# Weight splits in two halves of 1024 columns with a signal each, in a four-block transformer kernel on one core

## The reference, cut to what matters

```python
def hierarchical_moe(h, w_group, b_group, w_expert, b_expert, w_gate, w_up, w_down):
    ...
        gate = jnp.einsum('td,edf->tef', xb, w_gate)
        up = jnp.einsum('td,edf->tef', xb, w_up)
        act = jax.nn.silu(gate) * up * cb[..., None].astype(xb.dtype)
        return jnp.einsum('tef,efd->td', act, w_down)
```

## Time and profile before

| | |
|---|---|
| median of 3 runs | 1689.23 us (1687.36 to 1690.05) |
| the profiled execution's own time | 1690.0 us |
| its span, first to last instruction | 1688.0 us |
| TensorE busy | 1531.2 us, 91% |
| VectorE busy | 1295.4 us, 77% |
| ScalarE busy | 995.6 us, 59% |
| mean granted clock of TensorE | 0.959 of full speed |
| read from HBM | 400.37 MB, 238 GB/s over the span |

### The profile page before, as it was taken

How to read it: one execution, slowest core, us unless ns; L and a number is a source line. 1 busy time by engine, 2 the same in 40 slices (tenths; PEclk the granted TensorE clock), 3 DMA queues, 4 the chain that set the end, 5 groups by cost and what they waited for, 6 DMA issues and landing times.

```text
span 1688.0 us, 20547 instructions
## 1 busy us (share of the span) xinstructions
PE 1531.2 (91%) x7230; PEld 1257.6 (75%) x7230; DVE 1295.4 (77%) x1578; ACT 995.6 (59%) x1126; POOL 95.7 (6%) x187
## 2 busy tenths in 40 slices
PE   5997999979898899979969999999798969999998
PEld 4776877858776678768857888788686758888786
DVE  6756899776657898874667899888675578988877
ACT  3543577644534666646345777767385437777665
POOL 4002000030022000000020000000000100000000
PEclk9998999979998999989988999999799979999999
DMA  9433599865434799844445999999542228999985
GB/s 315 141 106 115 184 335 339 287 219 179 139 118 150 261 328 346 285 159 141 150 153 181 368 352 360 357 317 349 170 144 75 87 92 291 358 362 358 360 301 211
DMA packets 282868, 402.77 MB, mean 239 GB/s; under 512 B 16026, under 2 KB 220538, under 8 KB 282512
## 3 DMA queue, kind: packets, MB, share of 16 engines
q1 hardware_dynamic: 273632, 381.99, 66.9%
q0 software_dynamic: 9136, 19.48, 3.7%
HBM read 400.37 MB, written 1.05 MB: 238 GB/s over the span
## 4 chain that ended last, share of the span: by engine, by line
PE 69%; DVE 15%; ACT 6%; DMA 4%; issue 4%; SPq 0%; DVEq 0%; ACTq 0%
PE bank L623 19%; PE bank L625 18%; PE bank L624 18%; DVE w_lo_at L1920 5%; ACT w_hi_at L1384 3%; PE bank L640 2%; DMA raw_at<-in_moe_w_up_dram 2%; PE bank L755 1%; DMA raw_at<-in_moe_w_down_dram 1%; PE bank L780 1%; PE bank L911 1%; DMA raw_at<-in_w_in_dram 1%; PE bank L665 1%; DVE t_lo_at L1927 1%; PE bank L667 1%
## 5 line engine op out<-in xcount | busy, mean ns | idle before, releaser
L1920 DVE TENSOR_TENSOR w_lo_at<-raw_at,w_hi_at 128x2048 fp32r<-128x2048 f32 (+1 forms) x365 | 828.3, 2274 | 156.3 <-ACT w_hi_at L1384 147.5
L1384 ACT ACTIVATE w_hi_at<-raw_at 128x2048 fp32r<-128x2048 f32 (+1 forms) x365 | 693.4, 1901 | 176.3 <-PE bank L625 123.1
L623 PE MATMUL bank<-w_hi_at,xs_hi_at 128*128 128x512 f32 x800 | 327.4, 409 | 25.7 <-DVE w_lo_at L1920 12.5
L625 PE MATMUL bank<-w_hi_at,xs_lo_at 128*128 128x512 f32 x800 | 318.1, 398 | 0.0
L624 PE MATMUL bank<-w_lo_at,xs_hi_at 128*128 128x512 f32 x800 | 316.1, 395 | 0.0
L623 PE MATMUL bank<-w_hi_at,t_hi_at 128*128 128x512 f32 (+3 forms) x528 | 210.1, 398 | 12.2 <-DVE t_lo_at L1927 5.2
L624 PE MATMUL bank<-w_lo_at,t_hi_at 128*128 128x512 f32 (+3 forms) x528 | 203.8, 386 | 0.0
L625 PE MATMUL bank<-w_hi_at,t_lo_at 128*128 128x512 f32 (+3 forms) x528 | 203.7, 386 | 0.0
L623 PEld LDWEIGHTS bank<-w_hi_at,xs_hi_at 128*128 128x128 f32 x800 | 152.9, 191 | 59.1 <-DVE w_lo_at L1920 17.2
L625 PEld LDWEIGHTS bank<-w_hi_at,xs_lo_at 128*128 128x128 f32 x800 | 152.6, 191 | 34.9
L624 PEld LDWEIGHTS bank<-w_lo_at,xs_hi_at 128*128 128x128 f32 x800 | 153.4, 192 | 30.7
(11 more groups left out here) (500 smaller groups left out, 1726.6 us busy)
## 6 DMA issues: line engine op xcount, KB each, us to landing
raw_at<-in_moe_w_dram SPq DMA_DIRECT2D x192, 512.0 KB, 5.3
raw_at<-in_moe_w_gate_dram SPq DMA_DIRECT2D x128, 512.0 KB, 5.1
raw_at<-in_moe_w_up_dram SPq DMA_DIRECT2D x128, 512.0 KB, 6.5
raw_at<-in_moe_w_down_dram SPq DMA_DIRECT2D x128, 512.0 KB, 5.3
raw_at<-in_w_in_dram SPq DMA_DIRECT2D x40, 512.0 KB, 6.0
raw_at<-in_a_w_in_dram SPq DMA_DIRECT2D x20, 512.0 KB, 4.7
raw_at<-in_w_out_dram SPq DMA_DIRECT2D x16, 512.0 KB, 4.2
raw_at<-in_ple_wg_dram SPq DMA_DIRECT2D x16, 512.0 KB, 4.8
```

Of the source, the lines that this page charges most:

```text
L623: pe.matmul(out, ah, bh, start=start, stop=False, skip_group_check=loose)
L625: return pe.matmul(out, al, bh, start=False, stop=stop, skip_group_check=loose)
L1384: act.activation(WH[:, s.part(), 0:width], RAW[:, s.slot(), 0:width], ACT.Copy).then_inc(hi_done, 1)
L1920: dve.tensor_tensor(WL[:, s.part(), 0:width], RAW[:, s.slot(), 0:width], WH[:, s.part(), 0:width].bitcast(F32), ALU.subtract).then_inc(spl ...
```

## The change

Each split is made in two operations of half the unit's columns, on ScalarE and on VectorE. `hi_done` and `split_done` become two signals each, one for either half. TensorE waits for the first half's signal where it waited for the unit, and for the second half's ahead of the unit's third chunk. SyncE waits for the second half's signal. The other users of units (`unit_by_channel`, `down`, `down_by_half`, the mixing of heads, the projection of `p`, `unit_kv`) are changed in the same way.

```diff
-        hi_done = sem("hi_done")
-        split_done = sem("split_done")
+        hi_half = [sem(f"hi_half{i}") for i in range(2)]
+        split_half = [sem(f"split_half{i}") for i in range(2)]
...
                 if not s.early(1 - RING):
-                    sp.wait_ge(split_done, s.count(1 - RING))
+                    sp.wait_ge(split_half[1], s.count(1 - RING))
...
             def unit_by_token(banks, chunk, first, last, w=512, mid=None, src=(TH, TL)):
                 hi, lo = src
-                pe.wait_ge(split_done, s.count(1))
+                pe.wait_ge(split_half[0], s.count(1))
                 for c in range(4):
                     if c == 2 and mid is not None:
                         mid()
+                    if c == 2:
+                        pe.wait_ge(split_half[1], s.count(1))
...
                 def up(e, half, x, cols=slice(0, P)):
-                    pe.wait_ge(split_done, s.count(1))
+                    pe.wait_ge(split_half[0], s.count(1))
                     for k in range(4):
+                        if k == 2:
+                            pe.wait_ge(split_half[1], s.count(1))
...
                 def down(p, e):
                     pe.wait_ge(*m.al.at(p, e))
-                    pe.wait_ge(split_done, s.count(1))
+                    pe.wait_ge(split_half[0], s.count(1))
                     for f in range(2):
+                        if f == 1:
+                            pe.wait_ge(split_half[1], s.count(1))
...
-                act.activation(WH[:, s.part(), 0:width], RAW[:, s.slot(), 0:width], ACT.Copy).then_inc(hi_done, 1)
+                for i in range(2):
+                    a = slice(i * width // 2, (i + 1) * width // 2)
+                    act.activation(WH[:, s.part(), a], RAW[:, s.slot(), a], ACT.Copy).then_inc(hi_half[i], 1)
...
-                dve.wait_ge(hi_done, s.count(1))
-                dve.tensor_tensor(WL[:, s.part(), 0:width], RAW[:, s.slot(), 0:width],
-                                  WH[:, s.part(), 0:width].bitcast(F32), ALU.subtract).then_inc(split_done, 1)
+                for i in range(2):
+                    a = slice(i * width // 2, (i + 1) * width // 2)
+                    dve.wait_ge(hi_half[i], s.count(1))
+                    dve.tensor_tensor(WL[:, s.part(), a], RAW[:, s.slot(), a],
+                                      WH[:, s.part(), a].bitcast(F32), ALU.subtract).then_inc(split_half[i], 1)
```

More of the change, by code:

```diff
@@ L1098, in _ @@
                 owner[5] = dve_ready.at(("conv", L))
-                pe.wait_ge(split_done, s.count(2))
+                pe.wait_ge(split_half[0], s.count(2))
                 claim(2, 3)
@@ L1117, in _ @@
                 for c in range(2):
+                    if c == 1:
+                        pe.wait_ge(split_half[1], s.count(1))
                     for j in range(2):
@@ L1249, in unit_kv @@
                     for c in range(2):
+                        if j == 0 and c == 1:
+                            pe.wait_ge(split_half[1], s.count(1))
                         for tb in range(TB):
```

## The result

| | before | with the change |
|---|---|---|
| median (range), us | 1687.48 (1686.67 to 1690.05), 6 runs | 1672.51 (1668.63 to 1682.67), 6 runs |
| ratio, 95% interval | | 0.992 [0.9896, 0.9944] |
| the profiled execution's own time, us | 1690.0 | 1681.1 |
| its mean granted clock of TensorE | 0.959 | 0.959 |

The change is faster, by 15 us in the medians and by some 13 us (0.8%) in the ratio. I had forecast 8 us.

A forecast was written before the change was run, and what follows sets the result against it. TensorE was taken as the bound, with some 157 us idle to win from. Direct waits 7.7 plus waits behind pairs 5.5 less fixed costs 1.2 gave 12.0 us; two thirds, 8.0, kept: 1681 us, range 1674 to 1688.

The forecast's parts named there:

- the times of a split: ScalarE's halves end at 1.06 and about 2.02 us after the load, VectorE's at 2.3 and 3.45; TensorE starts 1.9 earlier.
- The wait at 266.03: TensorE held 1.44 us until 266.03 by `w_lo` behind `gated`; this wait goes, the same in three such places.
- TensorE's direct waits: Weight loads waiting on `w_lo`, 22.6 us in 16 waits, fall to a third or less; 7.7 us won.
- the waits in mid-unit: Some 360 added TensorE waits ahead of a unit's second half cost 0; at 0.02 us each, 7 us.
- the cover in the expert passes: In the full stretch `act_lo` has 0.95 us of cover before TensorE's `down`, against 0.1 to 0.2 us of delay.
- become the bound: Rival: VectorE bounds the expert passes once a unit's added cost passes 0.24 us; 1695 us at 0.28; chance 0.08.
- ring of loads and splits: Last passes of blocks 2 and 3: a turn takes 11.4 us, TensorE's own pace, so a shorter split wins nothing.
- two thirds: Keep 8.0 of 12.0 us, as closed waits may return at softmax, layer norm or gather; that rival's chance 0.17.
- Fixed costs on the path: About a dozen splits ahead of serial work (router, layer norms) lose 0.1 us each: 1.2 us lost.
- the waits behind a pair: Work waiting behind a `w_hi` and `w_lo` pair (score maximum, `glu`, gather, loop exits) comes up to 0.8 us earlier: 5.5 us.
- The rule I weighed: Each added operation from SBUF pays its fixed cost again: about 2 us on the dozen splits, 1681.5 instead of 1681.
- more than the sum: Rival: all 12.0 us kept, plus 2.6 from waits at the dynamic passes' entries: 1675 us or less; chance 0.08.

The follow-up runs named there:

- the experiment above: Whole splits as in the kernel before, but TensorE waits a second time in mid-unit for the same signal: 0.9989 of before, 0.2 us at equal clock.
- the overlap: The change with TensorE waiting for whole splits, 1679.05 us, set beside the same with VectorE's first half waiting for ScalarE's second, 1701.78 us.
- the change's third set: The change run again, unaltered, on one chip with the kernel that waits for whole splits: median 1674.05 us, ratio 0.9912 to before.
- the change's first set: The change as first measured against the kernel before, 6 runs: median 1672.51 us, ratio 0.992.
- ScalarE whole: The change, but ScalarE splits in one operation; VectorE in halves, TensorE starting on the first: 1690.95 us, 1.001 of before.
- quarters: The change with four operations of 512 columns on each engine, four signals, TensorE waiting at each chunk: 1678.50 us, 0.9935 of before.

## Why the prediction was wrong in size

**Right: the times of a split.** I had VectorE's end at 3.45 us after the start of ScalarE's half, and the trace has 3.45. Halves in a row start 1.13 us apart (I said 1.14). The wait at 266.03 is gone: the weight load that answers to it, in the first expert behind `gated`, waits for nothing.

```profile
263.30 0.19 PEld L623 LDWEIGHTS bank<-w_hi_at,xs_hi_at 128*128 128x128 f32 x1
```

**Right: TensorE's direct waits.** I said a third of 22.6 us or less; it is 7.3. The long one behind the layer norm was to come 1.06 us earlier. It is as long as before (5.74 us at 725.48), because TensorE reaches it earlier too. But the first statistics of that layer norm start at 718.96 before:

```profile
718.96 1.28 DVE L2282 BATCH_NORM_STATS2 stats_at<-x_at 128x6 f32<-128x512 f32 x2
```

and at 708.48 after, where the load starts on the first half of the split at 724.20:

```profile
708.48 1.28 DVE L2301 BATCH_NORM_STATS2 stats_at<-x_at 128x6 f32<-128x512 f32 x2
...
724.20 2.36 DVE L1939 TENSOR_TENSOR w_lo_at<-raw_at,w_hi_at 128x1024 fp32r<-128x1024 f32 x2 [0.22 <-DVE rs_at L2001]
```

So the weight load comes 18.0 us behind the statistics before (736.97) and 17.0 after: the 1 us is there.

**Right: the waits in mid-unit and the cover in the expert passes.** At the middle of an `up` unit in block 2 the third chunk's first matmul starts 0.24 us after the one before it, and by itself the wait cost 0.2 us in all, good to 1.5 (the experiment above).

```profile
928.34 0.40 PE L625 MATMUL bank<-w_hi_at,xs_lo_at 128*128 128x512 f32 x1
928.58 0.39 PE L623 MATMUL bank<-w_hi_at,xs_hi_at 128*128 128x512 f32 x1
```

VectorE did not become the bound: 36.96 us of 40 against 36.64.

**Right: nothing to win in block 2.** I said of its ring of loads and splits "I count nothing there". Of the overlap's gain none is made there (the starts above), though the loads leave the chain. I had misread one thing about it: in the chain before, 13 of the 41 pieces of `w_lo` and 11 of some 30 of `w_hi` (of half a microsecond or more) stand in the last passes of blocks 2 and 3, a third and not nearly half.

**Wrong, the discount: "I choose two thirds".** I had summed 12.0 us and kept 8.0, since the won time might be lost again at a softmax or a layer norm close behind. Here are the starts of the copy of the gates again, before:

```profile
306.69 0.17 DVE L2234 COPY gate_sel_at<-gate_sel_at 128x8 f32<-128x8 f32 x1
...
666.10 0.17 DVE L2234 COPY gate_sel_at<-gate_sel_at 128x8 f32<-128x8 f32 x1
...
1105.82 0.16 DVE L2234 COPY gate_sel_at<-gate_sel_at 128x8 f32<-128x8 f32 x1
...
1596.53 0.17 DVE L2234 COPY gate_sel_at<-gate_sel_at 128x8 f32<-128x8 f32 x1
```

and in the profiled execution of the change's third set, whose own time is 1676.5 us:

```profile
302.52 0.17 DVE L2253 COPY gate_sel_at<-gate_sel_at 128x8 f32<-128x8 f32 x1
...
653.29 0.17 DVE L2253 COPY gate_sel_at<-gate_sel_at 128x8 f32<-128x8 f32 x1
...
1090.08 0.17 DVE L2253 COPY gate_sel_at<-gate_sel_at 128x8 f32<-128x8 f32 x1
...
1582.20 0.16 DVE L2253 COPY gate_sel_at<-gate_sel_at 128x8 f32<-128x8 f32 x1
```

The change is ahead by 4.2, 12.8, 15.7 and 14.3 us. The end is 13.5 ahead. By the dynamic pass of block 1 nearly everything is won, and almost nothing of it is handed back in the 1000 us behind that. (The clocks of these two executions are 0.959 and 0.961, which is 2.4 of the 13.5 us by the slope.) At equal clock the gain of the 18 runs is 1687.4-1674.4 = 13.0 us, and my sum without the discount was 12.0. The discount is 4 of the 8.7 us between the forecast, 1681.2, and the 1672.5 measured. The rest is clock (1.8), the kernel before, which came out at 1687.5 over six runs instead of 1689.2, and 1.0 of the sum.

**Wrong in the mechanism: the terms of that sum.** The 12.0 came near the 13.0 by luck, because three wrong terms balanced. The worst is the second:

- *Fixed costs on the path*, 1.2 us in my sum: 7.8 measured (13 by the ratio). I had named a dozen splits. With 41 pieces of `w_lo` and some 30 of `w_hi` on the chain before, 41 times 0.08 to 0.17 and 30 times 0.1 to 0.21 us would be 6.3 to 13.3. That each piece on the chain pays is argued, not shown, but it is the count that comes near.
- *What a shorter split gives to everyone behind it*, in my sum 5.5 us for the waits behind a pair and a part of the direct ones (some 9.5 us together, by what I expected of the overlap alone): the overlap gave 17.7 us. The runs show it as many small gains in the expert passes of blocks 0 and 1, where I had priced single places (three waits behind `gated`, one `glu`, the gathers and the loop exits): the overlap's lead grows by 6.2 us in the passes of block 1 alone (5.8 us at 535, 12.0 at 655). From the tables of block 2 (894.5 us) to its dynamic pass (1105.8) the change gains 1.8 us, and by the end of the block it has given them back.
- *Direct waits*, 7.7 us: the early start closed 9.1 us of them beside the overlap and 15.5 without it, and was worth 3 to 4 at equal clock. By that the fear that led me to two thirds was justified for this term, and for this one alone. Without the clock moved it was worth 6.9 (means of all sets), near the 7.7; see the clock below.

Together, at equal clock: +7.8 for the operations, -17.7 for the overlap, -3.1 for the early start (both sets that wait for whole splits taken together, 1677.5), so -13.0. With the clock left as it was the same means give +11.9, -19.7 and -6.9, so -14.7. The overlap is the largest term either way.

**The rest of the 15 us goes with TensorE's clock.** The 18 runs of the change have a mean granted clock of 0.9624, the 65 of before 0.9609. At 1.19 us per 0.001 that is 1.8 us, and the difference of the two clocks is itself uncertain by 0.0012. The profiled execution of the change's first set shows how it goes. In block 3's attention, at 1305 to 1320 us, first that execution, then that of the third set (windows; PEclk is the third column from the end):

```profile
1300.00:1305.00 5.00, 3.93 (x20) 2.48 (x19) 1.29 (x2) 2.97 (x4) 0.00 (x0) 1.00 0.64 208
1305.00:1310.00 5.00, 5.00 (x13) 3.02 (x14) 1.31 (x5) 0.00 (x0) 0.00 (x0) 0.54 0.00 0
1310.00:1315.00 5.00, 5.00 (x12) 2.60 (x11) 0.77 (x4) 2.08 (x8) 0.00 (x0) 0.50 0.00 0
1315.00:1320.00 5.00, 5.00 (x15) 3.81 (x15) 3.78 (x9) 1.67 (x7) 0.00 (x0) 0.60 0.00 0
```

```profile
1300.00:1305.00 5.00, 3.93 (x22) 2.95 (x20) 1.36 (x3) 2.10 (x4) 0.00 (x0) 1.00 0.61 210
1305.00:1310.00 5.00, 5.00 (x20) 2.86 (x20) 1.34 (x5) 0.88 (x1) 0.00 (x0) 1.00 0.00 0
1310.00:1315.00 5.00, 5.00 (x22) 3.48 (x22) 2.86 (x12) 2.10 (x9) 0.00 (x0) 1.00 0.00 0
```

TensorE is busy 5.00 us of 5 in both, but in the first at 0.50 to 0.54, the lower of its two levels (1.2 GHz), and gets through 25 matmuls in 10 us instead of 42. Ahead of it both had a stretch at 3.93 of 5 us. Five microseconds of the gain were lost there in that execution: it is ahead of before by 14.2 us at 1235 and by 9.1 at 1341, while the other one is 13.8 ahead at both. Why the clock falls in one execution and not in another of the same program is open. So is why the change has a higher mean than the same kernel waiting for whole splits (0.9624 against 0.9592, 17 runs). An early start does not always go with a high clock: with ScalarE whole it is 0.9602, with quarters 0.9602. That is why the early start is worth 3 to 7 us over all sets (8.7 in the medians of one), depending on whether its clock is counted.

**The rule I weighed.** By the form rows a split pays 0.15 us more on VectorE and 0.19 more on ScalarE. The Trainium skill, page "VectorE: DVE Perf Modes", section "The TRN2 errata", gives (N+151)/0.96 ns for the one and 224 cycles of fixed cost for the other, by my estimate 0.157 and 0.187 us, and the trace agrees; so does the quarters' 686 ns (691 by the formula). The rule prices the added operations alone, 2 us on a dozen splits as I used it. They cost 8, and what two engines in a row gain from smaller operations stood against it: 18 us.

**The range.** 1674 was too high a low end: I had given "more than the sum" 0.08, and a time of that size is what came, though not by what I named for it (the closed waits at the dynamic passes), but by the overlap and the clock.

## What to carry to other kernels

When two engines work on one tile in turn, cutting it in two and signalling each half shortens the pair by some two fifths of the first engine's time (0.78 of 1.91 us), and here that was worth more than letting TensorE start early. Two pieces were enough: three were no better here and four were worse. Cost each added operation for more places than one happens to know; the count of its kind on the chain came near here. And look for the gain where the bounding engine has small idle times all along, as in the passes of blocks 0 and 1, rather than in a list of single long waits. A chain whose lines change is not yet time won.

## What the runs showed of the hardware

- A weight load or matmul of TensorE that waits for a signal already given costs nothing that can be measured: 360 more waits, 0.2 us in 1687, good to 1.5.
- TensorE can stand at its lower clock level while it is busy all the time (0.50 for 5 us at 5.00 us busy), in one execution and not in the next of the same program. The spread of this kernel's times, 1682 to 1696 us before, follows for the larger part the mean granted clock, at 1.19 us per 0.001.
- Operations with satisfied waits start before the one ahead of them has ended: 2.36 us for two of VectorE's halves of 1.22, 2.01 for two of ScalarE's of 1.05.
